# First conv tap on ScalarE, the norm of OUT1 pair by pair and a tile later, transposes moved in the attention slots

## The reference

```python
h = rmsnorm(x, pre_mix_norm)
conv_in, q_lat, kv_lat, k_rope = split(h @ w_in)
a, g = split(conv_in)                              # 1024 channels each
u = a * sigmoid(g)
u = causal_depthwise_conv(u, conv_w, conv_b)       # 31 taps
u = silu(layernorm(u, conv_ln_g, conv_ln_b))
q, kv = rmsnorm(q_lat) @ w_uq, rmsnorm(kv_lat) @ w_ukv     # 8 heads, rope on 64 columns
attn = causal_attention(q, k, v)
mix = concat([rmsnorm(u, conv_out_norm), rmsnorm(attn, attn_out_norm)]) @ w_out
x = x + rmsnorm(mix, post_mix_norm)
```

## Time and profile before

| | |
|---|---|
| median of 3 runs | 2180.47 us (2179.82 to 2182.12) |
| the profiled execution, its time | 2179.17 us |
| its span, first to last instruction | 2177.5 us |
| TensorE busy | 2152.2 us, 99% |
| VectorE busy | 1447.3 us, 66% |
| ScalarE busy | 1112.1 us, 51% |
| granted clock of TensorE, mean | 0.996 |

### The profile page before, as it was taken

One profiled execution on the slowest core, in us unless ns is written; L12 is line 12 of the kernel. 1 busy time (PEld: TensorE's weight loads), 2 busy tenths in 40 slices (PEclk: granted clock), 3 DMA queues, 4 the chain that ended last, 5 costly groups with the idle time before them and its releaser, 6 DMA issues.

```text
span 2177.5 us, 28612 instructions
## 1 busy us (share of the span) xinstructions
PE 2152.2 (99%) x9938; PEld 1793.3 (82%) x9938; DVE 1447.3 (66%) x2011; ACT 1112.1 (51%) x1450; POOL 50.2 (2%) x59
## 2 busy tenths in 40 slices
PE   9999999999999999999999999999999999999999
PEld 7897778888888888888888878888888888888887
DVE  5899966667666766444555557567877787784443
ACT  6556665444444444444466436555666666653332
POOL 1000000000000000000000032000000000000000
PEclk9999999999999999999999999999999999999999
DMA  7665344666666666555555544456665666656665
GB/s 226 190 182 164 126 155 146 204 192 191 193 195 192 191 193 218 193 193 192 163 155 160 173 122 141 151 174 191 187 198 174 193 188 192 188 182 206 193 190 164
DMA packets 216369, 393.11 MB, mean 181 GB/s; under 512 B 13695, under 2 KB 58313, under 8 KB 216043
## 3 DMA queue, kind: packets, MB, share of 16 engines
q1 hardware_dynamic: 216123, 391.13, 58.7%
q10 hardware_dynamic: 176, 1.06, 0.2%
HBM read 390.04 MB, written 2.10 MB: 180 GB/s over the span
## 4 chain that ended last, share of the span: by engine, by line
PE 92%; DVE 5%; ACT 1%; issue 1%; DMA 0%; SPq 0%; POOL 0%; DVEq 0%; ACTq 0%; POOLq 0%
PE ps L536 29%; PE ps L538 29%; PE ps L537 29%; DVE cv L1815 2%; DVE w_lo L1706 2%; PE ps L552 1%; PE ps L572 0%; PE ps L1094 0%; PE ps L922 0%; PE ps L941 0%; ACT w_hi L1132 0%; DVE fac L2137 0%; DMA raw<-in_w_in 0%; PE ps L1026 0%; PE ps L931 0%
## 5 line engine op out<-in xcount | busy, mean ns | idle before, releaser
L1706 DVE TENSOR_TENSOR w_lo<-raw,w_hi 128x1024 fp32r<-128x1024 f32 (+2 forms) x761 | 899.1, 1190 | 620.5 <-ACT w_hi L1132 612.0
L1132 ACT ACTIVATE w_hi<-raw 128x1024 fp32r<-128x1024 f32 (+2 forms) x761 | 778.9, 1030 | 772.9 <-PE ps L538 732.4
L536 PE MATMUL ps<-w_hi,hT_hi 128*128 128x512 f32 (+2 forms) x2208 | 864.3, 391 | 8.4 <-DVE w_lo L1706 3.2
L538 PE MATMUL ps<-w_hi,hT_lo 128*128 128x512 f32 (+2 forms) x2208 | 854.3, 387 | 0.0
L537 PE MATMUL ps<-w_lo,hT_hi 128*128 128x512 f32 (+2 forms) x2208 | 853.6, 387 | 0.0
L536 PEld LDWEIGHTS ps<-w_hi,hT_hi 128*128 128x128 f32 x2208 | 416.1, 188 | 92.6 <-issue 9.1
L538 PEld LDWEIGHTS ps<-w_hi,hT_lo 128*128 128x128 f32 x2208 | 415.7, 188 | 79.8
L537 PEld LDWEIGHTS ps<-w_lo,hT_hi 128*128 128x128 f32 x2208 | 416.2, 188 | 76.2
L536 PE MATMUL ps<-w_hi,aT_hi 128*128 128x512 f32 x704 | 274.0, 389 | 0.0
L538 PE MATMUL ps<-w_hi,aT_lo 128*128 128x512 f32 x704 | 273.9, 389 | 0.0
L537 PE MATMUL ps<-w_lo,aT_hi 128*128 128x512 f32 x704 | 273.9, 389 | 0.0
(11 more groups left out here) (274 smaller groups left out, 1051.7 us busy)
## 6 DMA issues: line engine op xcount, KB each, us to landing
raw<-in_w_up SPq DMA_DIRECT2D x264, 512.0 KB, 4.0
raw<-in_w_down SPq DMA_DIRECT2D x160, 512.0 KB, 4.5
raw<-in_w_gate SPq DMA_DIRECT2D x88, 512.0 KB, 4.4
raw<-in_w_in SPq DMA_DIRECT2D x80, 464.0 KB, 3.5
raw<-in_w_out SPq DMA_DIRECT2D x64, 512.0 KB, 3.9
raw<-in_w_in SPq DMA_DIRECT2D x64, 256.0 KB, 3.5
raw<-in_w_in SPq DMA_DIRECT2D x24, 448.0 KB, 3.5
raw<-in_w_down SPq DMA_DIRECT2D x32, 256.0 KB, 3.0
```

The source lines that it names most:

```text
L536: pe.matmul(o, xh, wh, start=first, stop=False)
L538: mm = pe.matmul(o, xl, wh, start=False, stop=last)
L1132: act.activation(w_hi[:, s, :kc, :width], raw[:, s, :kc, :width], ACT.Copy).then_inc(hi_ready, 1)
L1706: dve.tensor_tensor(w_lo[:, s, :kc, :width], raw[:, s, :kc, :width], w_hi[:, s, :kc, :width].bitcast(F32), ALU.subtract).then_inc(lo_ready, 1)
```

## The change

- **First tap.** `cu_evac` on ScalarE gets two more operations: as soon as a block's `uT` is there, ScalarE computes the first tap with bias of its two channel chunks (`ACT.Identity` with scale and bias) and raises `conv_first`. VectorE keeps 30 taps a chunk, 240 in all. `SLOT_TAPS` of the last two slots become 3 and 2.
- **Norm.** `LN_MEAN`, `LN_VAR` and `LN_SPREAD` are one tile later (10, 13, 14); `MIX_VAR` stays 19. Two splits of `w_lo` stand ahead of the wait for the variance. Silu and rounding alternate by pairs of chunks, with one rounding of a tile behind each of the first three pairs, and VectorE's splits follow that order.
- **Slots.** TensorE: `attn1_T` of heads 0 and 1 ahead of the tile, `qpe_pairs(1, 7)` behind the tile of slot 2, `attn1_fill` of heads 6 and 7 behind the tile. ScalarE: `qpe_copy(1, 7)` behind `attn1_pT(0)`. VectorE: `attn1_lo` of heads 6 and 7 behind the slot's taps.

```diff
-BLOCK_TAPS = 2 * TAPS
+BLOCK_TAPS = 2 * (TAPS - 1)
-SLOT_TAPS = [2, 5, 6, 6] + [8] * 7 + [5, 4, 4]
+SLOT_TAPS = [2, 5, 6, 6] + [8] * 7 + [5, 3, 2]
-LN_MEAN, LN_VAR, LN_SPREAD, MIX_VAR = 9, 12, 13, 19
+LN_MEAN, LN_VAR, LN_SPREAD, MIX_VAR = 10, 13, 14, 19
...
@@ TensorE, slots
-                if s == 2:
-                    qpe_pairs(1, 7)
                 if 0 <= s - 1 < HEADS:
                     attn1_S(s - 1)
                 if 0 <= s - 2 < HEADS:
                     attn1_PT(s - 2)
-                if 0 <= s - 3 < HEADS:
+                if 0 <= s - 3 < HEADS - 2:
                     attn1_fill(s - 3)
+                if s < 2:
+                    attn1_T(s)
                 if s < 6:
                     ukv_tile(s + 2)
                 else:
                     out1_tile(s - 6)
-                if s < HEADS:
+                if HEADS - 2 <= s - 3 < HEADS:
+                    attn1_fill(s - 3)
+                if s == 2:
+                    qpe_pairs(1, 7)
+                if 2 <= s < HEADS:
                     attn1_T(s)
                 if 0 <= s - 2 < HEADS:
                     attn1_PV(s - 2)
@@ ScalarE, cu_evac
+                act.wait_ge(cu_free, b + 1)
+                act.wait_ge(gains_ready, 3)
+                for c in range(2 * b, 2 * b + 2):
+                    at = G_AT["conv_b"] + c
+                    act.activation(cv[:, c, :], uT[:, c, 0:SEQ], ACT.Identity, scale=convw[:, c:c + 1],
+                                   bias=gains[:, at:at + 1]).then_inc(conv_first, 1)
@@ ScalarE, slots
-                if s == 2:
-                    qpe_copy(1, 7)
...
                 if 0 <= s - 2 < HEADS:
                     attn1_pT(s - 2)
+                if s == 2:
+                    qpe_copy(1, 7)
@@ ScalarE, OUT1
-            hi_upto(T_OUT1 + LN_MEAN + 4)
+            hi_upto(T_OUT1 + LN_MEAN + 3)
...
-            for c in range(CC):
-                g, b = G_AT["conv_ln_g"] + c, G_AT["conv_ln_b"] + c
-                ins = act.activation(cv[:, c, :], cv[:, c, :], ACT.Silu, scale=gains[:, g:g + 1], bias=gains[:, b:b + 1])
-                if c == 3:
-                    hi_upto(T_OUT1 + 17)
-            ins.then_inc(ln_act, 1)
-            hi_upto(T_OUT1 + 18)
-            act.wait_ge(ln_act, 2)
-            for c in range(CC):
-                g = G_AT["conv_out_norm"] + c
-                ins = act.activation(hT_hi[:, c, :], cv[:, c, :], ACT.Copy, scale=gains[:, g:g + 1])
-                if c % 2 == 1:
-                    ins.then_inc(conv_hi, 1)
-                if c == 3:
-                    hi_upto(T_OUT1 + 19)
+            for p in range(CC // 2):
+                for c in range(2 * p, 2 * p + 2):
+                    g, b = G_AT["conv_ln_g"] + c, G_AT["conv_ln_b"] + c
+                    ins = act.activation(cv[:, c, :], cv[:, c, :], ACT.Silu, scale=gains[:, g:g + 1], bias=gains[:, b:b + 1])
+                ins.then_inc(silu_done, 1)
+                act.wait_ge(silu_done, p + 1)
+                for c in range(2 * p, 2 * p + 2):
+                    g = G_AT["conv_out_norm"] + c
+                    ins = act.activation(hT_hi[:, c, :], cv[:, c, :], ACT.Copy, scale=gains[:, g:g + 1])
+                ins.then_inc(conv_hi, 1)
+                if p < 3:
+                    hi_upto(T_OUT1 + LN_SPREAD + 4 + p)
             attn_half(3)
             act.activation(lnsq[:], cv[:], ACT.Square).then_inc(ln_act, 1)
+            hi_upto(T_OUT1 + LN_SPREAD + 7)
@@ VectorE, taps
-                    if k == 0:
-                        dve.wait_ge(cu_free, b + 1)
+                    j += 1
+                    if j == 1:
+                        dve.wait_ge(conv_first, c + 1)
...
@@ VectorE, slots
-                if 0 <= s - 3 < HEADS:
+                if 0 <= s - 3 < HEADS - 2:
                     attn1_lo(s - 3)
...
                 taps(SLOT_TAPS[s] - 2)
+                if HEADS - 2 <= s - 3 < HEADS:
+                    attn1_lo(s - 3)
@@ VectorE, OUT1
-            lo_upto(T_OUT1 + LN_MEAN + 4)
+            lo_upto(T_OUT1 + LN_MEAN + 3)
             dve.wait_ge(ln_act, 1)
             chunk_sum(lnsq)
+            lo_upto(T_OUT1 + LN_VAR + 2)
             dve.wait_ge(ln_mm, 2)
...
-            lo_upto(T_OUT1 + 18)
             for c in range(CC):
-                if c == 4:
-                    lo_upto(T_OUT1 + 19)
                 if c % 2 == 0:
+                    lo_upto(T_OUT1 + LN_SPREAD + 3 + c // 2)
                     dve.wait_ge(conv_hi, c // 2 + 1)
...
-            lo_upto(T_OUT1 + 20)
-            dve.wait_ge(ln_act, 3)
+            dve.wait_ge(ln_act, 2)
             chunk_sum(lnsq)
```

More of the change, by code:

```diff
@@ L251, in build @@
         u_ready, cu_ready, cu_free = sem("u_ready"), sem("cu_ready"), sem("cu_free")
-        conv_tap = sem("conv_tap")
+        conv_first, conv_tap, silu_done = sem("conv_first"), sem("conv_tap"), sem("silu_done")
         trig_arg, trig_abs, trig_done = sem("trig_arg"), sem("trig_abs"), sem("trig_done")
@@ L1804, in taps @@
                     j, c = divmod(k, 2)
-                    if k == 0:
-                        dve.wait_ge(cu_free, b + 1)
+                    j += 1
                     c += 2 * b
+                    if j == 1:
+                        dve.wait_ge(conv_first, c + 1)
                     w = convw[:, j * CC + c:j * CC + c + 1]
                     u = uT[:, c, j:j + SEQ]
[L1810 to L1813, removed]
+                    if j > 1:
                         dve.wait_ge(conv_tap, i - 1)
-                        ins = dve.scalar_tensor_tensor(out=cv[:, c, :], in0=u, scalar=w, in1=cv[:, c, :],
-                                                       op0=ALU.mult, op1=ALU.add)
-                    ins.then_inc(conv_tap, 1)
+                    dve.scalar_tensor_tensor(out=cv[:, c, :], in0=u, scalar=w, in1=cv[:, c, :],
+                                             op0=ALU.mult, op1=ALU.add).then_inc(conv_tap, 1)
                     tap[0] += 1
```

## The result

The changed kernel takes 2183.91 us (median of 20 runs, 2181.99 to 2185.12) against 2180.46 us (20 runs, 2178.94 to 2182.16): ratio 1.0015, 95% interval 1.0009 to 1.002. It is slower by 3.4 us, within the 0.2% that the prediction called "no change", but the interval lies above 1. The profiled execution took 2182.29 us for a span of 2180.6 us, 3.1 us more than before.

What follows compares the result with a forecast made beforehand. TensorE, busy 2152.2 of 2177.5 us, was taken as the bound. -3.0 at tile 19, +2.0 clock there and +3.2 clock in the slots gave +2.2: 2181.4 us profiled, 2182.7 median, range 2176.5 to 2186.5.

Steps and rivals of the forecast that it cites:

- First tap: Early GEMM: eight activations on ScalarE, 1.1 us four times, hide behind the GEMM; VectorE's taps drop from 248 to 240.
- Slots 0 to 2: Start of the slots: wait for kv_block(0) 0.6 us, gap ahead of S(1) 2.7 us, S(2) 1.36 us later at 214.48.
- slot 2, clock, 1.6: Behind the 2.7 us gap ahead of S(1): TensorE's lower clock costs 1.6 us, bounds 0 and 2.4.
- Slots 9 and 10: PV(7) waits 2.8 us instead of 1.1 for head 6's low part; 1.36 us lost, plus 1.6 of clock.
- Mean, variance, pairs: OUT1: mean, variance and first convolution tile without waits; 3.9 and 2.58 us of waits, 2.4 and 1.6 of clock won.
- Tile 19: Ahead of tile 19 TensorE waits 4.5 us for the sums of the squared silu; clock price 2.0, range 1.6 to 2.4.
- Sum: Tile 19's sums 3.0 us earlier, clock losses of 2.0 there and 3.2 in the slots: +2.2 us.
- (a): Rival: slot moves cost nothing, neither delays nor clock; -3.7 or -4.1, 2176.4 us; chance 0.12 together with the no-wait rival.
- (b): Rival: the clock holds in the slots, the sum without its 3.2: -1.0, 2179.5 us; chance 0.22.
- (c): Rival: lower clock lasts longer after each of three standstills; +4.2 to +5.4, about 2185.3 us; chance 0.22, 0.20 of it slower.
- (d): Rival: no wait at tile 19 because ScalarE finishes the pairs sooner; -4.3, 2176.2 us; chance 0.12 together with the free-slot-moves rival.

Runs made afterwards that it cites:

- the late sums: Changed kernel with the sums of the squared silu ahead of tile 22 instead of 19, splits of tiles 20 to 23 moved ahead; 2176.31 us.
- the filler at tile 19 only: Changed kernel with 19 calls of idle matmuls (about 4.3 us) on TensorE in its wait ahead of the sums of tile 19; 2178.92 us.
- short fillers: Changed kernel with idle matmuls on TensorE in three waits: 12 calls ahead of S(1), 13 ahead of PV(7), 19 ahead of tile 19's sums; 2177.58 us.
- the last kernel: Norm and first tap as changed, slots as before, silu-square sums at tile 22, plus three taps moved from ahead of the slots into later slots; 2168.9 us.

## Why the prediction held, and where its terms were off

**First tap: right.** Hidden in the early GEMM (ScalarE 52.5 to 56.7 us in 102, TensorE 101.92), and at its end worth the 1.95 us and its clock that the kernel with the tap back paid.

**Slots 0 to 2: the delays right, the clock wrong in size.** The wait for `kv` was 0.48 (0.6 taken), the gap 2.73 (2.7), S(2) at 214.61 (214.48). ScalarE has `qpe_copy` ahead of exp(1), as placed:

```profile
212.61 0.60 ACT L1306 ACTIVATE qpeT<-ps 128x512 f32<-128x512 f32 x1 [2.72 <-PE ps L714]
```

The term "slot 2, clock, 1.6" was mis-sized: it measured 0 in six profiles with this gap (the changed kernel twice, the slot moves only, the late sums, slots 9 and 10 undone, the filler at tile 19 only) and 1.62 in a seventh (the first tap back). Taking "a longer gap than 2.58 loses it" from one row was the weak step, and the text had said that the rows can't decide it. The slots alone even kept the clock behind 2.59 us ahead of tile 16, the place that the 2.58 came from.

**Slots 9 and 10: right.** Low part of head 6 behind six taps:

```profile
253.70 2.46 DVE L1821 SCALAR_TENSOR_TENSOR cv<-uT,convw,cv 128x256 f32<-128x256 f32 x6
256.08 0.47 DVE L1907 SCALAR_TENSOR_TENSOR hT_lo<-ps,gains,hT_hi 128x256 fp32r<-128x256 f32 x1
```

It starts at 256.08 (255.94), PV(7) at 256.70 (256.4), a wait of 2.92 (2.8), and the clock took 1.4 to 1.6 (1.6). The clock fell behind this wait in every profile that has it without a filler.

**Mean, variance, pairs: right.** No wait at L789. The chain from the product to the end of the chunk sum took what it was forecast to take, counted from the product's end: the fourth rounding ended 10.7 us later (10.7), the square 13.6 (13.7), the sum 16.1 (16.2). All of it is 2.0 us later than written, 1.6 of it the clock of slot 9, which the prediction had kept for its last line.

```profile
288.18 2.29 DVE L1954 TENSOR_TENSOR cv<-ps,cv 128x2048 f32<-128x2048 f32 x1 [0.41 <-PE ps L796]
...
306.13 0.43 DVE L1931 TENSOR_TENSOR lnsq<-lnsq 128x256 f32<-128x256 f32 x1
```

**Tile 19: the wait right (4.34, 4.5 forecast), the price of its clock too small.** It measured 2.80 in the trace of the changed kernel and 2.75 with the filler, where 2.0 was taken and 1.6 to 2.4 were the bounds. But it is no fixed price: from the sums to L572, against 36.03 before, the same wait of 4.3 us cost 2.80, 2.60 (its repetition), 2.67 (first tap back), 2.23 (slots 0 to 2 undone) and 1.69 (slots 9 and 10 undone), and 3.12 with the norm alone. The windows show why. The clock stands at 1.2 GHz for some 6.8 us in each of these profiles but the one with slots 9 and 10 undone, where it is 3.4. Most of these stretches begin while TensorE still waits, and only what lies behind the wait is paid, at about half its length. The stretch began 0.4 us before the wait ended with the norm alone, 1.0 in the changed kernel, and 2.2 with slots 0 to 2 undone. With slots 9 and 10 undone it began behind the wait. The windows in which it began, in the order norm alone, changed kernel, slots 0 to 2 undone (TensorE not busy, PEclk already below 1):

```profile
301.00:302.00 1.00, 0.00 (x1) 0.00 (x1) 0.97 (x3) 1.00 (x2) 0.00 (x0) 0.82 0.00 0
```

```profile
305.00:306.00 1.00, 0.00 (x0) 0.00 (x0) 0.96 (x2) 1.00 (x3) 0.00 (x0) 0.79 0.00 0
```

```profile
303.00:304.00 1.00, 0.00 (x0) 0.00 (x0) 0.81 (x1) 1.00 (x2) 0.00 (x0) 0.73 0.00 0
```

**Sum.** Forecast -3.0 + 2.0 + 1.6 + 1.6 = +2.2. Measured at L572: 306.61 - 307.70 = -1.09, which holds slot 9's clock of 1.6 already (-2.7 without it), and +2.80: +1.71. The two errors, 1.6 too much in slot 2 and 0.8 too little at tile 19, half cancelled. The forecast for the profiled execution was 2181.4 and it took 2182.29; the difference is 0.5 less in OUT1 and 1.4 more in a stage that the change does not touch. The median, 2183.91, lies 1.2 above the forecast 2182.7. The forecast carried the distance of the median from the profiled execution over from before (1.3 us); it was 1.6 after, and this with the 0.9 of the profiled execution makes the 1.2. So the mechanism was right and the closeness of the number owes something to luck.

**Rivals.** (a) fell: `qpe_copy` and the low part came where the queues put them, and half by half the moves cost 1.5 and 3.9 us (0.95 and 2.79 up to tile 19's sums, ahead of the clock that varied there). (b) was right for slot 2 and wrong for slot 9. (c) was right in size at tile 19 alone; its time, 2185.3, lies 1.4 above the measured median, nearly as close as the forecast. (d) fell: the wait came.

The Trainium skill ("TensorE: Matmul & The Clock Gate", Part 1: The HAM clock gate) has the clock's monitor run free of the kernel. The traces here agree: the price at tile 19 differed between two executions of the same kernel (2.80 and 2.60), the same wait of 2.7 us kept the clock in six profiles and lost it in one, and a wait of 1.95 us lost it ahead of L789 while waits of 1.92 to 1.95 us ahead of S(1) kept it in four.

**Open.** Why the medians of the kernel with slots 0 to 2 undone and of those with short fillers gained 2.2 to 2.4 us more than their traces do at L572 (with the filler at tile 19 only, the runs go from 2177.03 us at a mean clock of 0.999 to 2182.29 at 0.996, so losses of the clock differ from run to run; where is not shown), and whether the taps moved in the last kernel shorten anything. One profile for each kernel does not show in which executions the clock falls where.

## What to carry to other kernels

A stall of the engine that sets the end goes on along the chain: before counting a removed wait as won, follow the same chain to its next meeting with that engine. Here it was tile 19, which had been in time by 0.3 us only because TensorE had stood still, and moving that meeting by three tiles turned 2.6 us of gain into 9. Work moved behind a tile to fill a short wait needs its own buffer's release checked: two waits of 0.4 and 0.7 us became one of 2.9 with the clock behind it.

## What the runs showed of the hardware

TensorE's clock also falls while the engine counts as busy. In the second block, eight matmuls with 17 rows of weights (L863, in the changed kernel L867) start at 1123.36 us before and at 1125.07 after, and the windows of before, of after, and of the last kernel, where it stays up, show:

```profile
1127.00:1130.00 3.00, 3.00 (x9) 2.59 (x9) 2.88 (x5) 0.00 (x0) 0.00 (x0) 0.53 0.00 0
1130.00:1133.00 3.00, 3.00 (x14) 2.65 (x14) 3.00 (x5) 0.00 (x0) 0.00 (x0) 0.90 0.39 80
```

```profile
1127.00:1130.00 3.00, 3.00 (x7) 1.25 (x6) 0.75 (x2) 1.51 (x2) 0.00 (x0) 0.70 0.24 92
1130.00:1133.00 3.00, 3.00 (x9) 2.56 (x9) 2.96 (x5) 0.00 (x0) 0.00 (x0) 0.50 0.00 0
1133.00:1136.00 3.00, 3.00 (x11) 2.62 (x11) 2.28 (x4) 0.68 (x1) 0.00 (x0) 0.66 0.54 158
```

```profile
1118.00:1121.00 3.00, 3.00 (x15) 2.69 (x15) 2.82 (x5) 0.00 (x0) 0.00 (x0) 1.00 0.00 0
```

No profile shows a wait of TensorE around them, and in the eleven in which the clock falls it does so 2.3 to 4.5 us after the first of the eight starts. That these eight are the cause is argued from the place alone; no run changes them. All 14 profiles go by the time at 1.2 GHz in this place, whichever version ran. With none (three profiles) the rest behind L572 took 1832.3 to 1833.1 us, with some 3.4 us (four) 1833.6 to 1834.1, and with some 6.8 us (seven) 1835.2 to 1835.6. So a single profile of this kernel can be 3 us off from another for a reason behind the stage under study.
